# GpSimd makes two of the four low parts of the mixed activations in both feed-forward parts

## The reference, cut to what matters

```
swiglu(x, w_gate, w_up, w_down) = (silu(x @ w_gate) * (x @ w_up)) @ w_down
```

## Time and profile before

| what | us |
|---|---|
| time, median of 3 runs | 1835.09 (1834.06 to 1835.31) |
| time of the profiled execution | 1835.46 |
| its span | 1833.3 |
| TensorE matmuls busy | 1796.7 (98%) |
| VectorE busy | 1125.4 (61%) |
| ScalarE busy | 710.3 (39%) |
| GpSimd busy | 1288.4 (70%) |

### The profile page before, as it was taken

How to read it: one execution, slowest core, us unless ns; L and a number is a source line. 1 busy time by engine, 2 the same in 40 slices (tenths; PEclk the granted TensorE clock), 3 DMA queues, 4 the chain that set the end, 5 groups by cost and what they waited for, 6 DMA issues and landing times.

```text
span 1833.3 us, 28330 instructions
## 1 busy us (share of the span) xinstructions
PE 1796.7 (98%) x10236; PEld 1531.4 (84%) x10236; DVE 1125.4 (61%) x1741; ACT 710.3 (39%) x1337; POOL 1288.4 (70%) x1190
## 2 busy tenths in 40 slices
PE   9999999999999999999999999999999998999998
PEld 7888888878878799998888877798876768999886
DVE  5166674149974798886116767574454189888731
ACT  3111111137762366662014267553423255666001
POOL 7766666767777788887667865453772678888775
PEclk9999999999999999999999999999999999999999
DMA  5222223232223332325223211101321222323421
GB/s 187 95 89 92 92 92 138 92 127 80 80 73 111 116 114 93 116 95 202 95 84 112 98 64 46 66 29 42 119 92 46 92 92 93 115 95 114 162 103 69
DMA packets 25886, 179.36 MB, mean 98 GB/s; under 512 B 2864, under 2 KB 2992, under 8 KB 6704
## 3 DMA queue, kind: packets, MB, share of 16 engines
q1 hardware_dynamic: 24048, 168.31, 25.6%
q10 hardware_dynamic: 1728, 9.58, 1.4%
HBM read 171.58 MB, written 6.29 MB: 97 GB/s over the span
## 4 chain that ended last, share of the span: by engine, by line
PE 84%; DVE 8%; ACT 3%; issue 3%; POOL 2%; DMA 1%; DVEq 0%; ACTq 0%; POOLq 0%
PE bank L457 12%; PE bank L459 12%; PE bank L458 12%; PE bank L1216 6%; PE bank L1218 6%; PE bank L1217 6%; PE bank L1665 2%; PE bank L1664 2%; PE bank L1663 2%; PE bank L495 2%; PE bank L496 2%; PE bank L497 2%; DVE temps L1394 1%; PE bank L2066 1%; POOL weights_lo L350 1%
## 5 line engine op out<-in xcount | busy, mean ns | idle before, releaser
L350 POOL TENSOR_TENSOR weights_lo<-raw_weights,weights_hi 128x512 fp32r<-128x512 f32 (+4 forms) x416 | 558.7, 1343 | 41.2 <-ACT weights_hi L369 7.4
L348 POOL TENSOR_SCALAR weights_hi<-raw_weights 128x512 fp32r<-128x512 f32 (+4 forms) x392 | 270.2, 689 | 344.4 <-PE bank L459 178.2
L457 PE MATMUL bank<-x_hi,weights_hi 128*128 128x512 f32 x688 | 272.4, 396 | 1.2 <-DVE temps L1350 1.1
L458 PE MATMUL bank<-x_hi,weights_lo 128*128 128x512 f32 x688 | 268.2, 390 | 0.0
L459 PE MATMUL bank<-x_lo,weights_hi 128*128 128x512 f32 x688 | 268.1, 390 | 0.0
L457 PEld LDWEIGHTS bank<-x_hi,weights_hi 128*128 128x128 f32 x688 | 129.5, 188 | 29.3 <-DVE temps L1350 1.5
L458 PEld LDWEIGHTS bank<-x_hi,weights_lo 128*128 128x128 f32 x688 | 129.5, 188 | 27.4 <-issue 1.2
L459 PEld LDWEIGHTS bank<-x_lo,weights_hi 128*128 128x128 f32 x688 | 129.4, 188 | 27.2
L1218 PE MATMUL bank<-x_lo,weights_hi 128*128 128x256 f32 x432 | 122.2, 283 | 0.0
L1258 POOL TENSOR_TENSOR weights_lo<-temps,weights_hi 128x512 fp32r<-128x512 f32 x72 | 108.1, 1521 | 2.7 <-ACT weights_hi L1290 2.7
L1258 POOL TENSOR_TENSOR weights_lo<-raw_weights,weights_hi 128x512 fp32r<-128x512 f32 x72 | 97.6, 1360 | 13.3 <-ACT weights_hi L1290 13.0
(11 more groups left out here) (552 smaller groups left out, 5078.8 us busy)
## 6 DMA issues: line engine op xcount, KB each, us to landing
raw_weights<-in_ffn_seven SPq DMA_DIRECT2D x36, 1024.0 KB, 4.7
raw_weights<-in_a_ug SPq DMA_DIRECT2D x16, 1024.0 KB, 4.8
raw_weights<-in_b_in SPq DMA_DIRECT2D x12, 1024.0 KB, 4.8
raw_weights<-in_ffn_down SPq DMA_DIRECT2D x12, 1024.0 KB, 4.7
raw_weights<-in_ffn_down SPq DMA_DIRECT2D x7, 1408.0 KB, 5.9
raw_weights<-in_a_out SPq DMA_DIRECT2D x8, 1024.0 KB, 4.7
raw_weights<-in_ffn_up SPq DMA_DIRECT2D x8, 1024.0 KB, 4.7
raw_weights<-in_a_v SPq DMA_DIRECT2D x7, 1024.0 KB, 4.8
```

The source lines that it names most:

```text
L348: nc.gpsimd.tensor_scalar(hi, raw, 1.0, 0.0, ALU.mult, ALU.add).then_inc(S("units_hi"), 1)
L350: nc.gpsimd.tensor_tensor(lo, raw, hi.bitcast(F32), ALU.subtract).then_inc(units_ready, 1)
L457: nc.tensor.matmul(ps, wh, xh[:, k, :], start=k == 0, stop=False)
L458: nc.tensor.matmul(ps, wl, xh[:, k, :], start=False, stop=False)
```

## The change

The low parts of mixtures t = 2 and t = 3 (the third and fourth) are computed by a new GpSimd function with its own semaphore count; VectorE keeps t = 0 and 1. GpSimd does t = 2 after its four splits of plain round 2 and t = 3 after those of plain round 3, each after waiting for ScalarE's high part of that mixture. TensorE waits, for those two, only for ScalarE's moved copies, and the copies wait for GpSimd's low parts. GpSimd's four plain rounds of an FFN are written out without the hardware loop. The number of operations and the arithmetic are the same.

```diff
--- before.py
+++ after.py
@@ -169,7 +169,7 @@
     [("b_thr", KB), ("seven_hi", 2 * PRODUCTS * SEVEN)], [("b_a", KB), ("seven_kept", 2 * 3 * SEVEN)], [("b_scan", KB), ("seven_sums", 2 * 4 * SEVEN)],
     [("b_y", KB), ("seven_gates", 2 * SEVEN)], [("b_ix", KB), ("seven_joined", 2 * SEVEN)], [("b_bterm", KB), ("seven_lo_by_dve", 2 * SEVEN)],
     [("a_vn", KA), ("seven_lo", 2 * POOL_LOWS * SEVEN)], [("a_spatial", KA), ("seven_used", 2 * PRODUCTS * SEVEN)], [("b_tl", KB), ("kept_x", 5)],
-    *([(early, n)] + _members(kind, ("ffn1", each), ("ffn2", each)) for early, n, kind, each in (("b_a2", KB, "mixed_hi", 4), ("b_m2", KB, "mixed", 4), ("a_s_read", KA, "mixed_lo", 4), ("b_thi", KB, "moved", 2))),
+    *([(early, n)] + _members(kind, ("ffn1", each), ("ffn2", each)) for early, n, kind, each in (("b_a2", KB, "mixed_hi", 4), ("b_m2", KB, "mixed", 4), ("a_s_read", KA, "mixed_lo", 2), ("b_thi", KB, "moved", 2), ("a_gu", KA, "mixed_lo_by_pool", 2))),
     [("raw_first2", 16), ("spilled", 32)], [("raw_first3", 16), ("reloaded", 32)], [("x_in2", 16), ("raw_rest", 16)],
     [("b_mult", KB)] + _members("gained", ("ffn1", KD), ("ffn2", KD)),
     [("fx_o", FOXH), ("ma_o", 2 * MH)], [("fx_hi", FOXH // 2), ("ma_hi", 2 * MH)], [("fx_lo", FOXH // 2), ("ma_lo", 2 * MH)],
@@ -411,13 +411,15 @@
                             pool_gates_low(pool, r - 1, 1 - parity)
                     if first(r) and after_first:
                         after_first()
+                    if ph.name in ("ffn1_up", "ffn2_up") and r in (2, 3):
+                        pool_mixed_low(pool, ph.name[:4], r)
                 if ph.name == "a_v":
                     for r in range(ph.rounds):
                         body(r, r % 2, r // 2)
                         if r == 3:
                             pool_causal_w_s(pool)
                     continue
-                if ph.name == "b_out" or ph.name.endswith("_tail"):
+                if ph.name in ("b_out", "ffn1_up", "ffn2_up"):
                     for r in range(ph.rounds):
                         body(r, r % 2, r // 2)
                 else:
@@ -1225,10 +1227,10 @@
                     return lambda k: x[MIX_OF[p]][:, k, :]
 
                 def mixed_ready(t):
-                    if r == 0:
+                    if r == 0 and t < 2:
                         pe.wait_ge(*due(f"{f}_mixed_lo", t + 1))
-                        if t >= 2:
-                            pe.wait_ge(*due(f"{f}_moved", t - 1))
+                    elif r == 0:
+                        pe.wait_ge(*due(f"{f}_moved", t - 1))
 
                 pe_bank_read(pe, f, g, 1)
                 product(M1, up[:, A_HALF], plain(XH, 0, A_HALF), plain(XL, 0, A_HALF), True)
@@ -1248,6 +1250,10 @@
                 mixed_ready(3)
                 product(M4, up[:, A_HALF], mixed(MIX_H, M4), mixed(MIX_L, M4), False)
 
+        def pool_mixed_low(pool, f, t):
+            pool.wait_ge(*due(f"{f}_mixed_hi", t + 1))
+            nc.gpsimd.tensor_tensor(LOW_AT[t], MIX[t], MIX_H[t].bitcast(F32), ALU.subtract).then_inc(S(f"{f}_mixed_lo_by_pool"), 1)
+
         def pool_seven(pool, ph):
 
             for r in range(SEVEN):
@@ -1273,7 +1279,7 @@
 
         def act_move_low(act, f, t):
             act.wait_ge(units_used, PH[f"{f}_up"].used(HEAD - 1, 3))
-            act.wait_ge(*due(f"{f}_mixed_lo", t + 1))
+            act.wait_ge(*due(f"{f}_mixed_lo_by_pool", t - 1))
             nc.scalar.activation(MIX_L[t], LOW_AT[t].bitcast(F32), ACT.Copy).then_inc(S(f"{f}_moved"), 1)
 
         def act_seven_hi(act, ph, r, p):
@@ -1428,7 +1434,7 @@
             else:
                 dve_ffn_plain(dve, f, head, 0, 0)
             dve_ffn_plain(dve, f, head, 1, 1)
-            for t in range(4):
+            for t in range(2):
                 dve_mixed_low(dve, f, t)
             dve_ffn_plain(dve, f, head, 2, 2)
             dve.wait_ge(*due(f"{f}_yl", HEAD - 1))
```

## The result

The changed kernel takes 1837.47 us (median of 12, 1835.06 to 1841.42), the kernel before on the same chip 1834.82 (median of 12, 1831.68 to 1836.71). The ratio is 1.002 with a 95% interval of 1.0013 to 1.0028, so +2.4 to +5.1 us; the two medians differ by 2.65. The forecast was +4.0. The profiled span went from 1833.3 to 1836.9, +3.6.

What follows compares the result with a forecast made beforehand. TensorE carries 84% of the chain, so VectorE and GpSimd edits pay only where it waits. FFN1's +2.1 and FFN2's +1.9 sum to +4.0 us: 1839.1 against the median of 1835.09, range 1834.4 to 1843.5.

Steps and rivals of the forecast that it cites:

- The mechanism: VectorE and GpSimd alternate on all-SBUF operations; the shared time per FFN grows from 2.2 to 4.6 us.
- GpSimd's price: A GpSimd subtraction of 128x1024, a quarter, takes 2.41 us alone, 2.3 from the other engine's end.
- Rival (b): Faster: GpSimd's quarter shares no time with VectorE; -4.0 us, 1831.1; chance 0.07.
- forecast +2.1: FFN1's seven-rounds: VectorE 2.5 us later at M5's low part, so 4.1 us lost instead of 1.99.
- one sign of being wrong: FFN1's M5: a new pause of 0.5 us was forecast; no pause would mean the alternation is not strict.
- ScalarE's two pauses: First seven-round: TensorE waits for ScalarE's kept banks, 0.7 us before M6 and 1.3 before M3.
- The joins' cost: M4 of the first and second seven-rounds: TensorE waits for VectorE's join, 0.7 and 0.9 us.
- forecast +1.9: FFN2: two earlier stalls and the seven-rounds' pauses lose 8.1 us instead of 6.16.
- The start of the seven-rounds: FFN2: delayed by stalls of 1.9 us at the fourth plain round and 1.8 before M1.
- the 1.9: FFN2's fourth plain round: GpSimd waits for ScalarE's third high part, so TensorE stands 1.9 us with restart.
- (a): Gain and new waits cancel: +0 to +3 us, time 1835 to 1838; chance 0.33.
- (c): TensorE's clock falls if the pause at FFN2's fourth plain round reaches 3 us; 1842.7; chance 0.10.

Runs made afterwards that it cites:

- e7_idle_places: The change with FFN1's two low parts between GpSimd's units 1 and 2 of plain round 2, FFN2's two after its last splits; ratio 0.9991 to the kernel before.
- e9_left_out: The changed kernel with the third and fourth low parts made by no engine, ScalarE moving the mixtures themselves (wrong result); ratio 0.9964 to the kernel before.
- e2_ffn1_only: The change in FFN1 alone, FFN2's low parts all on VectorE; ratio 1.0006 to the kernel before.
- e6_first_and_fourth: The changed kernel, but in FFN2 GpSimd makes the first low part instead of the third, at the same place; ratio 1.0012 to the kernel before.
- e3_ffn2_only: The change in FFN2 alone, FFN1's low parts all on VectorE; ratio 1.0008 to the kernel before.
- e4_third_only: In both FFNs GpSimd makes only the third low part, VectorE the other three; ratio 0.9998 to the kernel before.
- e8_late_moves: All low parts on VectorE, plain rounds written out, ScalarE's two moved copies placed after the bank copy for M3; one run, 1833.82 us.
- e10_gap_and_fourth: The best version: FFN1's two low parts in GpSimd's gap in plain round 2, FFN2's fourth alone after its last splits; 1832.08 us against 1834.86, ratio 0.9986.
- e1_unroll: The kernel before with only GpSimd's plain rounds written out without the hardware loop, all low parts on VectorE; ratio 0.9998.
- e5_fourth_only: In both FFNs GpSimd makes only the fourth low part, after its splits of plain round 3; ratio 1.0006 to the kernel before.
- e11_and_order: e10_gap_and_fourth plus VectorE's M5 low part right after its first two sums and ScalarE's moved copies later; ratio 0.9997 to the kernel before.

## Why the prediction was right, and where a term was off

**The mechanism held.** The forecast rested on one reading: that operations between SBUF operands on VectorE and GpSimd take turns, so that a quarter moved from the one to the other leaves the shared time and comes back at GpSimd's price. The 0.16 us between the first low part and the join say it for the change. The two places of e7_idle_places, with 1.5 and 0.15 us for the same two operations, tell it from an account in which each engine has its own time, and so does e9_left_out, where GpSimd's quarters turn out to have cost 8.75 us. Rival (b), faster, rested on that account and falls with it. The Trainium skill (GPSIMD Engine Reference, 8. Key points) has that the two engines share SBUF interfaces, with contention where VectorE has two SBUF inputs. These runs agree and add what it costs: 2.77 us for an operation of 0.68.

**GpSimd's price** was taken as 2.41 alone, from a slope over 384 and 512 columns. It measured 2.41 (1505.76) and 2.34 (two in 4.67). VectorE's price of 1.22 was read from the row of a mixture, another operation of the same size, not of a low part. Half of the 4497 ns that the Trainium skill has for 2048 columns (GPSIMD Engine Reference, 3.1 Elementwise — side-by-side cycle accounting) is an estimate of 2.25, a little low.

**FFN1**: forecast +2.1, measured 2.04 (and 1.78 in e2_ffn1_only). The sum was right with parts that were not, and that is luck. The prediction named one sign of being wrong that came true: FFN1's M5 has no pause, where 0.5 stood. It read this sign as "the alternation is then not strict". The rows say otherwise: VectorE's sum beside the quarter ends at 644.92, 0.56 behind the quarter's end (644.36), and the two operations behind it take 1.78 each. What was off is the timing of what stands before it. GpSimd's splits and its second quarter end 0.3 to 0.5 us earlier than was reckoned (644.36 for 644.85), so VectorE ends M5's low part at 648.32 for 648.9, and TensorE starts M5 at 648.47, with some 0.1 us of delay. The other terms are read with their restarts: the four pauses are 2.76 us of the 4.03, and the rest is 0.25 to 0.3 for each. ScalarE's two pauses then cost 0.6 and 1.3, where 0.7 and 1.3 stood. The joins' cost 1.1 and 1.0, in the first and third round, where 0.7 and 0.9 stood for the first and second. The missing M5 and the joins that were too cheap cancel.

VectorE also waited once for a transfer, of the weights of the third seven-round. The prediction had reckoned only the second round's transfer, which was in time:

```profile
661.67 1.84 DVE L1400 TENSOR_TENSOR temps<-raw_weights 128x512 f32<-128x512 f32 x1 [0.71 <-DMA raw_weights<-in_ffn_seven]
```

This 0.71 does not make the pause at 679.68: e2_ffn1_only and e6_first_and_fourth, with the same FFN1, have no such wait and the same pause of 0.70 there (679.33 and 679.52).

**FFN2**: forecast +1.9, measured +1.62 (1.88 in e3_ffn2_only). The start of the seven-rounds was to come 3.7 us later and came 3.31: 1.51 and 1.24 of pause, some 1.8 and 1.5 with restarts, where 1.9 and 1.8 stood. Inside them 4.4 us of loss were forecast and 4.47 measured. The places of the pauses were right up to ScalarE's: the fourth plain round by GpSimd's split, M1 by its low part, M5 at 0.59 for 0.85. Those of the joins came in the second and third round instead of the first and second. The high part that starts it came as the row of ScalarE says,

```profile
1504.64 1.04 ACT L1278 ACTIVATE x_mixed_hi<-x_mixed 128x1024 fp32r<-128x1024 f32 x1
```

and ended 6.83 us after the third plain round's start; forecast was 6.9 (1503.8 less 1496.86). That high part was taken to be what makes the 1.9 a loss. This step was only half right: e6_first_and_fourth took its wait away and kept 0.6.

**The rivals.** By the time alone (a), that gain and new waits cancel, could not be told from the forecast: its 1835 to 1838 hold 1837.47, and the forecast's own 1837.6 to 1841.1 just miss it. The trace decides. Both waits before M1 and the plain round came, and FFN1's loss doubled; only in one place was (a) right, FFN1's M5. (c), the lower clock, was tied to a pause of 3 us at the fourth plain round; it came to 1.51 and left the granted clock at 1.00, by this stretch of the changed kernel (the columns of the earlier trace rows):

```profile
1511.50:1514.00 2.50, 2.46 (x11) 2.07 (x12) 2.33 (x4) 0.63 (x1) 2.42 (x2) 1.00 0.03 7
```

Its price of 2.3 us for a fall was also too high: the last section has one at 1.6 to 1.7.

**What stays open.** That FFN1's two quarters add up and FFN2's two do more is argued from the cover above, not shown by a run of its own. The join's pauses move between the first, second and third round from kernel to kernel, even between two kernels with the same FFN1, and what sends them there was not tried. The 0.8 us between the best version's trace and its median lie inside the interval.

## What to carry to other kernels

Before moving work from a busy engine to one with idle time, ask whether they share what the work uses: here VectorE and GpSimd take turns on SBUF operands. In each FFN 2.2 us of work left the one and came back as 4.7 on the other (two quarters of 2.34 to 2.41 alone), and the kernel became 3.7 us longer by the trace. Look for a place in which both are idle (FFN1's gap gave 1.5 us, FFN2's 0.15), and put nothing that waits for a late producer in front of work that TensorE needs. And where one engine's chain sets the end of a round, taking away the pauses of the others only moves them: 1.3 us of ScalarE's pauses removed were worth nothing, 2.4 of those for GpSimd 0.6.

## What the runs showed of the hardware that I had not expected

The length of a pause does not say whether TensorE's clock falls behind it. Before FFN1 it stands 3.1 us for VectorE in every kernel. In the changed kernel the granted clock is then 0.57 and 0.58 in two stretches of 2 us, so near the lower level of 1.2 GHz, and 1.00 from 620; in the best version it stays at 2.4 GHz. These are the first stretch of the changed kernel, then that of the best version:

```profile
616.00:618.00 2.00, 1.81 (x2) 0.79 (x3) 0.73 (x2) 0.00 (x0) 0.00 (x0) 0.57 0.03 12
```

```profile
616.00:618.00 2.00, 1.90 (x5) 0.94 (x6) 0.64 (x2) 0.00 (x0) 2.00 (x2) 1.00 0.00 0
```

From the end of that pause to the first seven-product matmul it is 30.76 us in the former (616.19 to 646.95) and 29.04 in the latter (616.10 to 645.14). Of the thirteen profiled kernels three have some 29.05 (e4_third_only, e8_late_moves and e10_gap_and_fourth; the second has VectorE and GpSimd as before in this part), the other ten 30.5 to 30.8. So 1.6 to 1.7 us of a single span can be this alone (in e8_late_moves against e1_unroll, 29.05 against 30.69, nothing in this part differs but the clock), as large as each FFN's share of the change. That is why the figures of the experiments start behind the pause, and why their spans were not compared. The two spans of the result may be: in both the clock had fallen here (30.69 and 30.76 us).

At M5 of FFN2 it is the other way round: the best version's clock fell behind a pause of 1.88, and that of e7_idle_places stayed behind one of 1.89 (the best version first):

```profile
1519.00:1521.00 2.00, 2.00 (x11) 2.00 (x12) 2.00 (x3) 1.57 (x4) 2.00 (x2) 0.56 0.00 0
```

```profile
1519.00:1521.00 2.00, 1.44 (x12) 1.48 (x12) 2.00 (x4) 0.95 (x2) 2.00 (x2) 1.00 0.00 0
```

There a fall costs little: e5_fourth_only has the same FFN2 edit without a fall, and its stretch is 209.04 against 209.21. The falls in the FFN2 of e6_first_and_fourth and e11_and_order stand at such a place too. The likely reason, by the waits above, is that with a fall the join, not TensorE, sets when M4 starts.

The other surprise is how exactly the two engines' turns show: in the changed kernel a VectorE operation ends 0.54 to 0.56 us after the GpSimd quarter beside it (1508.17 to 1508.72, 1522.26 to 1522.80, 644.36 to 644.92), the 0.55 that the trace before gave.
